# Four feed-forwards in two phases: all up tiles, then all down tiles with 512-column products over eight banks

## The chip, the core and the metric

The kernel runs on one core of a Trainium2 chip. A core has a matrix engine (TensorE), VectorE, ScalarE, GpSimd, and SyncE, which here issues the loads. The time is the device time of one execution in microseconds. A smaller time is better.

## What is computed

Two transformer blocks on 256 tokens of width 1024, in f32. The first has two gated feed-forwards (inner width 2816), a mixer of several attentions and a cross attention to a memory; the second has an RWKV-7 layer and a windowed attention, each with a squared-ReLU feed-forward (inner width 4096). Cut to what matters here:

```python
def swiglu(h, w_gate, w_up, w_down):
    return (jax.nn.silu(h @ w_gate) * (h @ w_up)) @ w_down

def squared_relu_mlp(h, w1, w2):
    return jnp.square(jax.nn.relu(h @ w1)) @ w2

def first_block(...):
    x = x + 0.5 * swiglu(rmsnorm(x, ffn1_norm), ffn1_w_gate, ffn1_w_up, ffn1_w_down)
    x = x + hybrid_mixer(rmsnorm(x, mix_norm), ...)
    x = x + memory_cross_attention(rmsnorm(x, mem_q_norm), rmsnorm(mem, mem_kv_norm), ...)
    x = x + 0.5 * swiglu(rmsnorm(x, ffn2_norm), ffn2_w_gate, ffn2_w_up, ffn2_w_down)
    return rmsnorm(x, final_norm)

def second_block(...):
    for i in range(2):
        out = rwkv7_time_mix(...) if i == 0 else swa_layer(rms_norm(x, ln_mix[1]), k_sh, v_sh, ...)
        x = x + out
        x = x + squared_relu_mlp(rms_norm(x, ln_mlp[i]), mlp_w1[i], mlp_w2[i])
        if i == 0:
            k_sh, v_sh = shared_kv(x, kv_norm, w_kv, k_gain)
    return x

```

## The kernel before

All activations stand transposed on chip: 128 channels on the partitions, 8 chunks of channels (`KC`), 256 tokens (`SEQ`) along the free axis. All weights come as one stream of 1 MB tiles of 128 x 2048 f32, in the order of use, through a ring of four (`feed`, L266, on SyncE's queue). A matmul reads `fp32r`, which keeps only a part of the bits, so every operand is split in two: ScalarE copies half a tile to `tile_hi` (L305, `heads_after`), VectorE subtracts to `tile_lo` (L315, `rests_after`). Four halves have room (`SPLIT`); a half is split again when TensorE has used the half four before. `may_split` decides from the tile number that a call is given how far a splitter may go at that place, so the calls `heads_before`, `rests_after` and the like are what sets the order of both engines.

`product` (L353 to L357) makes one product of a 128 x 128 weight block with 256 tokens in three matmuls of 256 columns: high by high, high weights by low activations, low weights by high activations. Each matmul loads its own weights. A tile holds 16 products.

`ffn_stage` runs four times: `ffn1` and `ffn2` (gated, 22 up tiles and 11 down tiles), `mlp1` and `mlp2` (squared ReLU, 16 and 16). A step `j` makes 256 inner values: one up tile (`col_to_T`; gated: two) into a PSUM bank. In the gated stages VectorE multiplies by the token scale (L768, L771), ScalarE applies SiLU (L726), VectorE multiplies both (L774). In the others ScalarE applies ReLU (L731) and VectorE scales (L780) and squares (L781). Then ScalarE writes the high part (L736), VectorE the low part (L789). They go to one of three slots (`depth`), of which the first begins at another offset (`AT_FIRST_SLOT` 128, the others `AT_MOVING` 160, modulo 256 bytes). The down tile of step `j` comes `LAG` = 2 steps later (`row_to_T`) and adds into banks 4 to 7, two chunks of 256 columns in each:

```python
            for j in range(steps):
                ...
                if j >= LAG:
                    down(j - LAG)
            mark_tail(e)
            for j in range(steps - LAG, steps):
                down(j)
```

The last down tile finishes the output chunks pair by pair. `tail_vector` adds each pair to the residual in one operation (L514, or L516 with the factor 0.5), ScalarE writes the high part for the next stage (L548) and the squares (L554), VectorE the low part (L524). `first_to_T` of the next stage waits for two chunks at a time (`x_arrives`), then `scale_sums` and `scale_spread` bring the token scale in.

## Time and profile before

| what | value |
|---|---|
| median of 3 runs | 1413.38 us (1409.81 to 1413.94) |
| the profiled execution, span | 1422.4 us |
| TensorE busy (matmul) | 1372.8 us, 97% |
| VectorE busy | 913.7 us, 64% |
| ScalarE busy | 706.0 us, 50% |
| HBM read | 219.55 MB, 155 GB/s over the span |
| matmuls | 12692 |

The profiled execution has no other time of its own than the span, from the first to the last instruction; it is 9.0 us above the median of the runs. Matmuls overlap in the records (one lasts 280 ns and the next starts 113 to 118 ns later), so a busy TensorE says little, and starts are what to compare.

### The profile page before, as it was taken

The page shows a single profiled execution, that of the slowest core. Times are in us where ns is not written, and L with a number is a line of the kernel's source. Part 1 is how long each engine was busy: PE and PEld are TensorE (multiplying, and loading weights), DVE is VectorE, ACT ScalarE, POOL GpSimd, SP SyncE. Part 2 cuts the span into 40 slices and gives each one's busy share as a digit, 9 for nine tenths or more (in the row PEclk, how much of TensorE's full clock was granted, in tenths as well). Part 3 has the DMA queues.
Part 4 walks back from the last instruction along what each step waited for, and adds up shares of the span by engine and source line. Part 5 has one row for each costly group of instructions (what it writes and reads, how often), then busy time and mean ns, then how long its engine had stood idle before and what let it go on. Part 6 is the DMA issues. An engine that isn't in the chain of part 4 may idle for free. (4 is left out here: it accounts for less than half of the span.)

```text
span 1422.4 us, 28871 instructions
## 1 busy us (share of the span) xinstructions
PE 1372.8 (97%) x12692; PEld 1314.1 (92%) x12692; DVE 913.7 (64%) x1419; ACT 706.0 (50%) x1098; POOL 8.2 (1%) x14
## 2 busy tenths in 40 slices
PE   7999999999899999999999899999999996999999
PEld 7999999888799999999998677889999995999999
DVE  4665566557785546666588763667666668666664
ACT  5444455356564446444458333446444466554442
POOL 0000000000000000000000010000000000000000
PEclk9999999999999999999999998999999999999999
DMA  7555555461344344655524021114555541255552
GB/s 272 208 179 191 194 180 179 182 264 60 119 178 178 129 151 156 214 182 197 199 85 176 31 91 60 61 60 167 190 197 207 190 149 60 94 204 178 178 184 84
DMA packets 33109, 222.48 MB, mean 156 GB/s; under 512 B 3879, under 2 KB 5295, under 8 KB 6616
## 3 DMA queue, kind: packets, MB, share of 16 engines
q1 hardware_dynamic: 31928, 219.57, 42.7%
q8 instruction: 100, 1.64, 0.4%
q10 hardware_dynamic: 1056, 1.07, 0.2%
q14 instruction: 25, 0.20, 0.0%
HBM read 219.55 MB, written 1.07 MB: 155 GB/s over the span
## 5 line engine op out<-in xcount | busy, mean ns | idle before, releaser
L315 DVE TENSOR_TENSOR tile_lo<-ring,tile_hi 128x1024 fp32r<-128x1024 f32 x388 | 466.0, 1222 | 276.8 <-ACT tile_hi L305 276.2
L305 ACT ACTIVATE tile_hi<-ring 128x1024 fp32r<-128x1024 f32 x388 | 399.5, 1053 | 250.8 <-PE ps L357 245.8
L355 PE MATMUL ps<-hT_hi,tile_hi 128*128 128x256 f32 x1664 | 467.5, 281 | 5.0 <-DVE tile_lo L315 1.8
L356 PE MATMUL ps<-hT_lo,tile_hi 128*128 128x256 f32 x1664 | 463.4, 278 | 0.0
L357 PE MATMUL ps<-hT_hi,tile_lo 128*128 128x256 f32 x1664 | 463.4, 278 | 0.0
L355 PEld LDWEIGHTS ps<-hT_hi,tile_hi 128*128 128x128 f32 x1664 | 315.0, 189 | 10.6 <-issue 4.6
L356 PEld LDWEIGHTS ps<-hT_lo,tile_hi 128*128 128x128 f32 x1664 | 312.9, 188 | 0.0
L357 PEld LDWEIGHTS ps<-hT_hi,tile_lo 128*128 128x128 f32 x1664 | 312.7, 188 | 0.0
L355 PE MATMUL ps<-hidden_hi,tile_hi 128*128 128x256 f32 x864 | 241.2, 279 | 0.0
L357 PE MATMUL ps<-hidden_hi,tile_lo 128*128 128x256 f32 x864 | 241.2, 279 | 0.0
L356 PE MATMUL ps<-hidden_lo,tile_hi 128*128 128x256 f32 x864 | 241.2, 279 | 0.0
L355 PEld LDWEIGHTS ps<-hidden_hi,tile_hi 128*128 128x128 f32 x864 | 163.5, 189 | 0.0
L356 PEld LDWEIGHTS ps<-hidden_lo,tile_hi 128*128 128x128 f32 x864 | 162.4, 188 | 0.0
L357 PEld LDWEIGHTS ps<-hidden_hi,tile_lo 128*128 128x128 f32 x864 | 162.3, 188 | 0.0
L736 ACT ACTIVATE hidden_hi<-hidden_whole 128x512 fp32r<-128x512 f32 x54 | 34.2, 633 | 114.1 <-DVE hidden_whole L774 65.8
L789 DVE TENSOR_TENSOR hidden_lo<-hidden_whole,hidden_hi 128x512 fp32r<-128x512 f32 x54 | 37.4, 692 | 39.3 <-ACT hidden_hi L736 26.2
L780 DVE TENSOR_TENSOR hidden_whole<-gate,token_scale 128x512 f32<-128x512 f32 x32 | 22.1, 692 | 32.4 <-ACT gate L731 32.4
L731 ACT ACTIVATE gate<-ps 128x512 f32<-128x512 f32 x32 | 19.0, 595 | 42.8 <-PE ps L357 42.8
L1064 ACT ACTIVATE scores<-scores,lane_stats 128x128 f32<-128x128 f32 (+3 forms) x80 | 35.4, 445 | 8.8 <-DVE lane_stats L1090 8.8
L355 PE MATMUL ps<-y_turned,tile_hi 128*128 128x256 f32 x128 | 35.8, 280 | 2.9 <-DVE tile_lo L315 2.9
L726 ACT ACTIVATE gate<-gate 128x512 f32<-128x512 f32 x22 | 13.9, 632 | 46.1 <-DVE gate L768 46.1
L356 PE MATMUL ps<-y_turned,tile_hi 128*128 128x256 f32 x128 | 35.4, 277 | 0.0
(467 smaller groups left out, 1997.5 us busy)
## 6 DMA issues: line engine op xcount, KB each, us to landing
ring<-stream SPq DMA_DIRECT2D x204, 1024.0 KB, 4.8
x_sb<-x SPq DMA_DIRECT2D x4, 256.0 KB, 4.0
bias<-f_dram ACTq DMA_DIRECT2D x1, 1024.0 KB, 8.1
fox_bias<-forget_dram SPq DMA_DIRECT2D x1, 1024.0 KB, 6.2
squares<-mem SPq DMA_DIRECT2D x1, 1024.0 KB, 4.7
out<-x_sb SPq DMA_DIRECT2D x4, 256.0 KB, 2.2
const_sb<-const SPq DMA_DIRECT2D x1, 581.0 KB, 9.8
small_sb<-small SPq DMA_DIRECT2D x1, 493.5 KB, 9.5
```

What stands on the lines that cost most here:

```text
L305: act.activation(e.w_hi[:, n % SPLIT, :], e.ring[:, tile % RING, span(n % 2, HALF)], ACT.Copy).then_inc(e.tile_hi.handle, 1)
L315: dve.tensor_tensor(e.w_lo[:, n % SPLIT, :], e.ring[:, CUT[n // 2] % RING, span(n % 2, HALF)], e.w_hi[:, n % SPLIT, :].bitcast(F32), ALU.s ...
L355: pe.matmul(out, left[0], right[0], start=start, stop=False)
L356: pe.matmul(out, left[0], right[1], start=False, stop=False)
L357: return pe.matmul(out, left[1], right[0], start=False, stop=stop)
L726: act.activation(tmp[:, j % 2, :], tmp[:, j % 2, :], ACT.Silu).then_inc(*act_done.one())
L731: act.activation(tmp[:, j % 2, :], e.ps[:, up_bank(j, 0), :], ACT.Relu).then_inc(*act_done.one())
L736: act.activation(slot(0, j), whole[:, j % 2, :], ACT.Copy).then_inc(*hi_ready.one())
L780: link.done(dve.tensor_tensor(halves_of(both), halves_of(tmp[:, j % 2, :]), scale_pairs(e), ALU.mult))
L789: dve.tensor_tensor(slot(1, j), both, slot(0, j).bitcast(F32), ALU.subtract).then_inc(*hidden_ready.one())
L1064: x = act.activation(summed(step)[:, lane], summed(step)[:, lane], ACT.Exp, bias=st[:, 0, lane:lane + 1], accum_out=st[:, 1, lane:lane + 1])
```

## The change

- Each feed-forward now runs all its up tiles and then all its down tiles, in the program and in the weight stream (`lay_out_stream`).
- The inner values of all steps stay on chip, in one tensor `hidden` at `AT_MOVING`, the high and low part of a step 2048 bytes apart.
- A down product is `wide_product`: one matmul of 512 columns (high weights by both parts of the activations) and one of 256 (low weights by the high part). Each of the 8 output chunks has a PSUM bank of its own, whose halves are summed at the end.
- The residual add therefore takes two operations per pair of chunks, the second waiting for the first.
- Up tiles rotate over four banks; the first down tile takes the banks in the order in which they were last used. `mlp2` starts its rotation at bank 4 (`first=2`). The key, value and query products after `mlp1` move to other banks.
- Pairs of high and low parts are now one tensor each with views (`Pair`), so `tile_hi` and `tile_lo` are `tile_pair`, `hT_hi` and `hT_lo` are `hT_pair`.

```diff
+    return pe.matmul(out, left.lo, right.hi, start=False, stop=stop)
+
+
+def wide_product(pe, bank, left, right, start, stop):
+
+
+
+    def low(stop):
+        return pe.matmul(bank[:, 0:SEQ], left.lo, right.hi, start=False, stop=stop)
+
+    if stop:
+        low(False)
+    mm = pe.matmul(halves_of(bank), left.hi, right.both, start=start, stop=stop)
+    return mm if stop else low(False)
 
 
...
-def add_to_residual(e, dve, b, scale, last_tile, bank=4):
+def add_to_residual(e, dve, b, scale, last_tile, bank=4, wide=False):
 
     if b < 3:
         dve.wait_ge(*e.sig("acc_ready").since(b + 1))
     else:
         multiplied(e, dve, last_tile)
+    if wide:
+        xs = e.x[:, two(b), :]
+        for half in range(2):
+            x = dve.scalar_tensor_tensor(out=xs, in0=e.ps[:, pair_of(b), span(half, SEQ)], scalar=scale, in1=xs,
+                                         op0=ALU.mult, op1=ALU.add)
+            if half == 0:
+                Chain(dve, e.sig("dve_step")).done(x)
+        x.then_inc(*e.sig("residual_added").one())
+        return
     xs = e.x[:, two(b), :].rearrange("p m n -> p (m n)")
     if scale == 1.0:
...
+def pair_of(n, first=0):
+
+    at = 2 * ((n + first) % 4)
+    return slice(at, at + 2)
+
+
+def bank_of(m, first=0):
+    return pair_of(m // 2, first).start + m % 2
+
...
+            first_to_T(e, pe, g0, hT, up_bank(0))
+            col_to_T(e, pe, g0 + 1, hT, up_bank(1), between=lambda: scale_sums(e, pe, scale_bank))
+            scale_spread(e, pe, scale_bank)
+            for n in range(2, count):
+                if n >= 4:
+                    pe.wait_ge(*emptied.at(n - 3))
+                col_to_T(e, pe, g0 + n, hT, up_bank(n))
+
+            def down(w, k, j, m, start=False, stop=False):
+                return wide_product(pe, e.ps[:, bank_of(m), :], cut(w, ALL, span(m, P)), chunk(j, k), start, stop)
+
+            halves = [arrived(e, pe, down0, k) for k in range(2)]
+            pe.wait_ge(*hidden_ready.at(1))
+            up_last = [max([-1] + [n for n in range(count) if up_bank(n) == bank_of(m)]) for m in range(KC)]
+            for m in sorted(range(KC), key=lambda m: up_last[m]):
+                pe.wait_ge(*(emptied.at(up_last[m] + 1) if up_last[m] >= 0 else e.sig("scale_ready").at(1)))
+                for k in range(2):
+                    mm = down(halves[k], k, 0, m, start=k == 0)
+            mm.then_inc(*e.tile_done.one(2))
+            for j in range(1, steps - 1):
                 pe.wait_ge(*hidden_ready.at(j + 1))
-                row_to_T(e, pe, down_tile(j), hid[j % depth], 0, j == 0, j == steps - 1)
-
-            for j in range(steps):
-                if gated and j >= 2:
-
-                    pe.wait_ge(*hidden_ready.at(j - 1))
-                if not gated and j >= 4:
-
-                    pe.wait_ge(*act_done.at(j - 3))
-                for which in range(per - 1):
-                    nth = (per - 1) * j + which
-                    if nth == 0:
-                        first_to_T(e, pe, up_tile(j, which), hT, up_bank(j, which))
-                    elif nth == 1:
-                        col_to_T(e, pe, up_tile(j, which), hT, up_bank(j, which), between=lambda: scale_sums(e, pe, 7))
-                        scale_spread(e, pe, 7)
-                    else:
-                        col_to_T(e, pe, up_tile(j, which), hT, up_bank(j, which))
-                if j >= LAG:
-                    down(j - LAG)
+                for k in range(2):
+                    w = arrived(e, pe, down0 + j, k)
+                    for m in range(KC):
+                        mm = down(w, k, j, m)
+                    mm.then_inc(*e.tile_done.one())
             mark_tail(e)
-            for j in range(steps - LAG, steps):
-                down(j)
+            pe.wait_ge(*hidden_ready.at(steps))
+            halves = [arrived(e, pe, end, k) for k in range(2)]
+            for m in range(KC):
+                for k in range(2):
+                    mm = down(halves[k], k, steps - 1, m, stop=k == 1)
+                if m % 2 == 1 and m < KC - 1:
+                    mm.then_inc(*e.sig("acc_ready").one())
+            mm.then_inc(*e.tile_done.one(2))
 
         @block.scalar
         def _(act):
             heads_after(e, act, 2 * (g0 + 1))
             scale_root(e, act)
-            scale_copy(e, act, 7)
+            scale_copy(e, act, scale_bank)
+
...
+                    tile_after(e, act, g0 + j)
                     if j >= 2:
...
+                heads_after(e, act, 2 * (g0 + ups * (j + 1)))
                 act.wait_ge(*whole_ready.at(j + 1))
...
-                both = whole[:, j % 2, :]
+                rests_before(e, dve, g0 + ups * j + 1)
...
+                    dve.tensor_tensor(gate[:, j % 2], halves_of(e.ps[:, up_bank(2 * j), :]), scale_pairs(e),
+                                      ALU.mult).then_inc(*consumed.one())
+                    rests_after(e, dve, 2 * (g0 + 2 * j) + 2)
+                    tile_after(e, dve, g0 + 2 * j + 1)
+                    dve.tensor_tensor(whole[:, j % 2], halves_of(e.ps[:, up_bank(2 * j + 1), :]), scale_pairs(e),
+                                      ALU.mult).then_inc(*consumed.one())
+                    dve.wait_ge(*consumed.at(2 * j + 2))
                     dve.wait_ge(*act_done.at(j + 1))
-                    x = dve.tensor_tensor(both, both, tmp[:, j % 2, :], ALU.mult)
+                    dve.tensor_tensor(whole[:, j % 2], whole[:, j % 2], gate[:, j % 2], ALU.mult).then_inc(*whole_ready.one())
...
+                    link.done(dve.tensor_tensor(whole[:, j % 2], gate[:, j % 2], scale_pairs(e), ALU.mult))
+                    dve.tensor_tensor(whole[:, j % 2], whole[:, j % 2], whole[:, j % 2], ALU.mult).then_inc(*whole_ready.one())
+                rests_after(e, dve, 2 * (g0 + ups * (j + 1)))
                 dve.wait_ge(*hi_ready.at(j + 1))
...
     link = Chain(e.nc.vector, e.sig("dve_step"))
     KEYS = -1
-    banks = {KEYS: 0, 0: 1, 1: 2, 2: 7, 3: 5}
...
 
     heads_of = lambda n: 2 if n == KEYS else 4
@@ -3241,8 +3283,8 @@
             act.activation(s.q[:, PAIRS, :], e.ps[:, 0, 0:SEQ], ACT.Copy)
             act.activation(s.key_squares[:, :], e.ps[:, 0, 0:SEQ], ACT.Square).then_inc(*squared.one())
             return
-        act.activation(flat(s.q[:, two(n), :]), e.ps[:, 1 + n, :], ACT.Copy)
-        act.activation(flat(e.sq[:, two(n), :]), e.ps[:, 1 + n, :], ACT.Square).then_inc(*squared.one())
+        act.activation(flat(s.q[:, two(n), :]), e.ps[:, query_bank[n], :], ACT.Copy)
+        act.activation(flat(e.sq[:, two(n), :]), e.ps[:, query_bank[n], :], ACT.Square).then_inc(*squared.one())
 
     def sums_at(n):
         return e.ps[:, 7 if n == KEYS else 6, span(order[n], TT * 4)].rearrange("p (t h) -> p t h", t=TT)[:, :, 0:heads_of(n)]
...
-        tiles.extend(downs[-LAG:])
+        tiles.extend(downs)
 
     def cols(w, columns=None):
         tiles.extend(col_tiles(w, np.arange(w.shape[1]) if columns is None else columns))
```

TensorE, ffn1, the place where the first down tile begins. Before (step 0's down tile, behind the sixth up tile):

```order
L355 MATMUL ps<-hT_hi,tile_hi 128x256
L356 MATMUL ps<-hT_lo,tile_hi 128x256
L357 MATMUL ps<-hT_hi,tile_lo 128x256
L355 MATMUL ps<-hidden_hi,tile_hi 128x256
L356 MATMUL ps<-hidden_lo,tile_hi 128x256
L357 MATMUL ps<-hidden_hi,tile_lo 128x256
L355 MATMUL ps<-hidden_hi,tile_hi 128x256
L356 MATMUL ps<-hidden_lo,tile_hi 128x256
L357 MATMUL ps<-hidden_hi,tile_lo 128x256
```

After (behind the 22nd up tile; L386 is the wide matmul, L382 the low one, L372 to L374 are `product`):

```order
L372 MATMUL ps<-hT_pair,tile_pair 128x256
L373 MATMUL ps<-hT_pair,tile_pair 128x256
L374 MATMUL ps<-hT_pair,tile_pair 128x256
L386 MATMUL ps<-hidden,tile_pair 128x512
L382 MATMUL ps<-hidden,tile_pair 128x256
L386 MATMUL ps<-hidden,tile_pair 128x512
L382 MATMUL ps<-hidden,tile_pair 128x256
```

Three matmuls of 256 columns for each product have become one of 512 and one of 256.

VectorE, the middle of mlp2: the hidden operations (L780, L781, L789; after: L832, L833, L836) and the splits of weight tiles (L315; after: L331). Before:

```order
L315 TENSOR_TENSOR tile_lo<-ring,tile_hi 128x1024 x4
L780 TENSOR_TENSOR hidden_whole<-gate,token_scale 128x512
L781 TENSOR_TENSOR hidden_whole<-hidden_whole 128x512
L789 TENSOR_TENSOR hidden_lo<-hidden_whole,hidden_hi 128x512
L315 TENSOR_TENSOR tile_lo<-ring,tile_hi 128x1024 x4
L780 TENSOR_TENSOR hidden_whole<-gate,token_scale 128x512
L781 TENSOR_TENSOR hidden_whole<-hidden_whole 128x512
L789 TENSOR_TENSOR hidden_lo<-hidden_whole,hidden_hi 128x512
```

After:

```order
L331 TENSOR_TENSOR tile_pair<-ring,tile_pair 128x1024
L832 TENSOR_TENSOR hidden_whole<-gate,token_scale 128x512
L833 TENSOR_TENSOR hidden_whole<-hidden_whole 128x512
L331 TENSOR_TENSOR tile_pair<-ring,tile_pair 128x1024
L836 TENSOR_TENSOR hidden<-hidden_whole,hidden 128x512
L331 TENSOR_TENSOR tile_pair<-ring,tile_pair 128x1024
L832 TENSOR_TENSOR hidden_whole<-gate,token_scale 128x512
L833 TENSOR_TENSOR hidden_whole<-hidden_whole 128x512
L331 TENSOR_TENSOR tile_pair<-ring,tile_pair 128x1024
L836 TENSOR_TENSOR hidden<-hidden_whole,hidden 128x512
L331 TENSOR_TENSOR tile_pair<-ring,tile_pair 128x1024
```

A step had four splits, for its up and its down tile; it now has two, one of them ahead of the low part, and the splits of all down tiles come behind the last step.

VectorE, the end of ffn1: residual adds (L516; after: L547) and low parts of the next input (L524; after: L565). Before:

```order
L315 TENSOR_TENSOR tile_lo<-ring,tile_hi 128x1024 x5
L516 SCALAR_TENSOR_TENSOR x_sb<-ps,x_sb 128x512 x3
L524 SCALAR_TENSOR_TENSOR hT_lo<-x_sb,small_sb,hT_hi 128x256 x2
L516 SCALAR_TENSOR_TENSOR x_sb<-ps,x_sb 128x512
L524 SCALAR_TENSOR_TENSOR hT_lo<-x_sb,small_sb,hT_hi 128x256 x6
L315 TENSOR_TENSOR tile_lo<-ring,tile_hi 128x1024 x2
```

After:

```order
L331 TENSOR_TENSOR tile_pair<-ring,tile_pair 128x1024 x20
L547 SCALAR_TENSOR_TENSOR x_sb<-ps,x_sb 128x512 x6
L565 SCALAR_TENSOR_TENSOR hT_pair<-x_sb,small_sb,hT_pair 128x256 x2
L547 SCALAR_TENSOR_TENSOR x_sb<-ps,x_sb 128x512 x2
L565 SCALAR_TENSOR_TENSOR hT_pair<-x_sb,small_sb,hT_pair 128x256 x6
L331 TENSOR_TENSOR tile_pair<-ring,tile_pair 128x1024 x2
```

The splits of all eleven down tiles stand in a row ahead of the adds, and each add has become two.

## Rows read from the trace of the kernel before

**Rows 1.** The page, part 1: busy us, share of the span, instructions.

```profile
PE 1372.8 (97%) x12692; PEld 1314.1 (92%) x12692; DVE 913.7 (64%) x1419; ACT 706.0 (50%) x1098; POOL 8.2 (1%) x14
```

**Rows 2.** Waits of TensorE: us in total, times, longest us.

```profile
PE ps L355 <- DVE tile_lo L315: 7.0, 8, 1.5
```

**Rows 3.** Timeline, TensorE, stage mlp1: start us, us.

```profile
1069.92 0.28 PE L355 MATMUL ps<-hidden_hi,tile_hi 128*128 128x256 f32 x1
...
1074.00 0.28 PE L355 MATMUL ps<-hidden_hi,tile_hi 128*128 128x256 f32 x1
...
1080.12 0.28 PE L355 MATMUL ps<-hidden_hi,tile_hi 128*128 128x256 f32 x1
...
1084.34 0.28 PE L355 MATMUL ps<-hidden_hi,tile_hi 128*128 128x256 f32 x1
```

**Rows 4.** Timeline, TensorE, stage ffn1.

```profile
118.02 0.28 PE L355 MATMUL ps<-hidden_hi,tile_hi 128*128 128x256 f32 x1
...
122.26 0.28 PE L355 MATMUL ps<-hidden_hi,tile_hi 128*128 128x256 f32 x1
```

**Rows 5.** Windows of ffn1, ffn2, mlp1, mlp2: us, busy (x) by engine, PEclk, DMA.

```profile
100.00:140.00 40.00, 40.00 (x342) 40.00 (x341) 24.66 (x26) 17.11 (x19) 0.00 (x0) 1.00 0.52 185
640.00:680.00 40.00, 40.00 (x354) 40.00 (x353) 24.07 (x24) 16.84 (x19) 0.00 (x0) 1.00 0.58 210
1040.00:1080.00 40.00, 40.00 (x353) 40.00 (x352) 25.59 (x26) 19.10 (x22) 0.00 (x0) 1.00 0.55 197
1320.00:1360.00 40.00, 40.00 (x341) 40.00 (x340) 23.33 (x25) 18.20 (x22) 0.00 (x0) 1.00 0.53 194
```

**Rows 6.** Timeline, TensorE, stage mlp2.

```profile
1263.29 0.28 PE L357 MATMUL ps<-hT_hi,tile_lo 128*128 128x256 f32 x1
1263.46 0.38 PE L355 MATMUL ps<-hT_hi,tile_hi 128*128 128x256 f32 x1
```

**Rows 7.** Timeline, TensorE, the key/value tile after mlp1.

```profile
1143.07 0.33 PE L355 MATMUL ps<-kvT_hi,tile_hi 128*128 128x256 f32 x1
...
1144.09 0.33 PE L355 MATMUL ps<-kvT_hi,tile_hi 128*128 128x256 f32 x1
```

**Rows 8.** Timeline, TensorE, memory projection.

```profile
427.79 0.41 PE L357 MATMUL ps<-memT_hi,tile_lo 128*128 128x256 f32 x1
...
428.86 0.41 PE L356 MATMUL ps<-memT_lo,tile_hi 128*128 128x256 f32 x1
```

**Rows 9.** Window around it.

```profile
427.00:431.00 4.00, 4.00 (x23) 4.00 (x23) 1.67 (x4) 0.71 (x2) 0.00 (x0) 0.58 0.72 262
```

**Rows 10.** Groups by line and form, TensorE: xcount, busy us, mean ns.

```profile
L1817 PE MATMUL ps<-mem_kv,fox_bias 128*128 128x256 f32 x32 | 7.1, 381 | 0.8 <-ACT fox_bias L1855 0.8
...
L1281 PE MATMUL ps<-bias,flip_sb 128*128 128x512 f32 x8 | 3.6, 592 | 0.0
```

**Rows 11.** The page, part 5, VectorE.

```profile
L315 DVE TENSOR_TENSOR tile_lo<-ring,tile_hi 128x1024 fp32r<-128x1024 f32 x388 | 466.0, 1222 | 276.8 <-ACT tile_hi L305 276.2
...
L780 DVE TENSOR_TENSOR hidden_whole<-gate,token_scale 128x512 f32<-128x512 f32 x32 | 22.1, 692 | 32.4 <-ACT gate L731 32.4
```

**Rows 12.** Timeline, VectorE, two hidden operations of ffn1.

```profile
101.22 0.69 DVE L771 TENSOR_TENSOR hidden_whole<-ps,token_scale 128x512 f32<-128x512 f32 x1 [0.45 <-PE ps L357]
101.95 0.69 DVE L774 TENSOR_TENSOR hidden_whole<-hidden_whole,gate 128x512 f32<-128x512 f32 x1
```

**Rows 13.** Timeline, ScalarE's last split and VectorE's adds, end of ffn1.

```profile
197.44 1.06 ACT L305 ACTIVATE tile_hi<-ring 128x1024 fp32r<-128x1024 f32 x1 [1.73 <-PE ps L357]
...
199.68 1.28 DVE L516 SCALAR_TENSOR_TENSOR x_sb<-ps,x_sb 128x512 f32<-128x512 f32 x2
...
202.29 0.87 DVE L524 SCALAR_TENSOR_TENSOR hT_lo<-x_sb,small_sb,hT_hi 128x256 fp32r<-128x256 f32 x2
```

**Rows 14.** Timeline, TensorE, first matmul after ffn1.

```profile
203.31 0.36 PE L355 MATMUL ps<-hT_hi,tile_hi 128*128 128x256 f32 x1 [0.25 <-DVE hT_lo L524]
```

**Rows 15.** Timeline, VectorE, last add of ffn2.

```profile
717.45 0.69 DVE L516 SCALAR_TENSOR_TENSOR x_sb<-ps,x_sb 128x512 f32<-128x512 f32 x1 [0.67 <-PE ps L357]
```

More of the change, by code:

```diff
@@ L368, in cut @@
 def cut(pair, *index):
-    return tuple(part[index] for part in pair)
+    both = None if pair.both is None else pair.both[(index[0], slice(None), *index[1:])]
+    return Pair(pair.hi[index], pair.lo[index], both)
 ALL = slice(None)
@@ L656, in ffn_stage @@
     steps = width // 256
-    per = 3 if gated else 2
+    ups = 2 if gated else 1
     g0 = FIRST[section]
-    depth = 3
-    act_done, whole_ready, hi_ready, hidden_ready, scaled, chain = (
-        e.sig(x) for x in ("gate_ready", "hidden_whole_ready", "hidden_hi_ready", "hidden_ready", "gate_scaled", "dve_step"))
-    hT = e.hT
-    def up_tile(j, which):
-        return g0 + (per - 1) * j + max(j - LAG, 0) + which
-    def down_tile(j):
-        return g0 + (per - 1) * min(j + LAG + 1, steps) + j
@@ L670, in up_bank @@
-    def up_bank(j, which):
-        return 2 * (j % 2) + which if gated else (0, 2, 1, 3)[j % 4]
-    end = down_tile(steps - 1)
+    count = ups * steps
+    down0, end = g0 + count, g0 + count + steps - 1
+    consumed, act_done, whole_ready, hi_ready, hidden_ready, chain = (
+        e.sig(x) for x in ("gate_scaled", "gate_ready", "hidden_whole_ready", "hidden_hi_ready", "hidden_ready", "dve_step"))
+    emptied = consumed if gated else act_done
+    hT = e.hT
+    scale_bank = bank_of(4, first)
@@ L675, in ffn_stage, with chunk @@
     all_squared = e.sig("squared").since(4)
+    up_bank = lambda n: bank_of(n % 4, first)
     with Open(nc) as block, ExitStack() as stack:
-        hid = [e.pair(stack, f"hidden{n}", [P, 2, SEQ], AT_MOVING if n else AT_FIRST_SLOT) for n in range(depth)]
-        whole = e.sb(stack, f"hidden_whole{nc.next_id()}", [P, 2, 2 * SEQ])
-        tmp = e.sb(stack, f"gate{nc.next_id()}", [P, 2, 2 * SEQ])
-        def slot(part, j):
-            return hid[j % depth][part][:, :, :].rearrange("p m n -> p (m n)")
+        hidden = e.sb(stack, f"hidden{nc.next_id()}", [P, steps, 2, 2, SEQ], F32R, AT_MOVING)
+        whole = e.sb(stack, f"hidden_whole{nc.next_id()}", [P, 2, 2, SEQ])
+        gate = e.sb(stack, f"gate{nc.next_id()}", [P, 2, 2, SEQ])
+        def chunk(j, c):
+            return Pair(hidden[:, j, 0, c, :], hidden[:, j, 1, c, :], hidden[:, j, :, c, :])
```

119 lines of the change are left out of this document (50 added, 69 removed).

## The prediction

> **What bounds the kernel now.** I read the page first. TensorE is busy 97% of the span, VectorE 64%, ScalarE 50% [rows 1]. Busy time says little of pipelined matmuls, so I asked the waits next: inside the four feed-forwards TensorE waits for almost nothing (8 waits for a split tile, 7.0 us in the whole program [rows 2]). The bound there is the rhythm of the matmuls themselves, and the timeline gives it. I take starts of equal matmuls, 12 products (36 matmuls) apart.
>
> That shows **two rhythms at one clock**. In the first squared-ReLU stage 12 products take 4.08 us: 340.0 ns a product, 113.3 ns a matmul [rows 3]. In the first gated stage the same instructions take 4.24 us: 353.3 ns, 117.8 ns a matmul [rows 4]. Windows of 40 us, one per stage, tell which stage runs how: about 342 matmuls is the slow rhythm, 354 the fast one, all at clock 1.00, that is 2.4 GHz [rows 5]. So ffn1 and mlp2 were slow, ffn2 and mlp1 fast. The rhythm changes only where TensorE stops for a moment: in mlp2 it went from fast to slow at 1263.46 after a hiccup of some 60 ns [rows 6]. I call it a draw, made anew at each stop. Products from hidden slot 0, which lies at another offset, take 351.7 ns in a fast stage (4.22 us for 12) [rows 3]; in a slow one they hardly stand out.
>
> **Why 113 and not 107?** 256 columns at 2.4 GHz are 106.7 ns. In the key/value tile, three matmuls of 256 columns alternate with six of 128: nine take 1.03 us, 114 ns each, though their columns would need 71 ns on average [rows 7]. Their one common cost is a weight load each. And where a stream is long enough to cover a load, the surcharge goes: at 427 us, at half clock, matmuls of 256 columns stand 214 ns apart (1.07 us for 5), which is 256 columns at 1.2 GHz and nothing more [rows 8, 9]. So a load of 128 columns takes about 111 to 114 ns, and a 256-column stream at full clock just fails to cover it.
>
> **The change part by part.** *Wide down products.* Each of 864 down products (11, 11, 16, 16 tiles of 16) drops one weight load and one instruction; columns stay 768. The 512-column matmul should cost its stream, 214 ns by [rows 8], since it covers the next load. The low one keeps 113.3. Together 328 ns. The bounds: 320 (768 columns at 2.4 GHz) below, and above 353.3, if 512 columns cost two slow matmuls. Far off stands the one 512-column row of this kernel, plain f32: it lasts 592 ns, one of 256 columns 381 [rows 10]. 211 ns for 256 columns more would make 422 of 512, but that is twice the fp32r rhythm already at 256, so I read from it only that time goes with columns. I take 328, by the row that is nearest in mechanism. By stage, from this profile: ffn1 176 products x 25.3 = 4.5 us; ffn2 112 x 12.0 + 64 of slot 0 x 23.7 = 2.9; mlp1 160 x 12.0 + 96 x 23.7 = 4.2; mlp2 256 x 25.3 = 6.5. **Sum -18.1 us.** In the fast stages slot 0's penalty (64 x 11.7 = 0.7 and 96 x 11.7 = 1.1 us) is part of it, as every hidden part now lies at the good offset.
> The Trainium skill ("TensorE: Matmul & The Clock Gate", on the measured gap) states N/2.4 + 2.5 ns back to back: 216 and 109, a product of 325 and a sum of -20.7. It would have today's product at 328, and the rows say 340 to 353, so the measurement decides.
>
> *Up tiles in a row.* Same matmuls, same tiles, same bytes (a 1 MB tile per 5.4 to 5.7 us). VectorE has the tighter budget in the squared-ReLU stages: before, three hidden operations per 11 us, now per 5.4. Two splits (1.22 us) and three operations (0.69) are 4.5 us, and the ReLU must be awaited some 0.85 us after the tile's end: 5.3 of 5.4 us [rows 11]. The split awaited is needed a whole tile later, so I cost it at nothing; the cover is 5.4 us of slack, and if it went, each of 32 tiles would show a stop. The gated stages use 7.3 of 11 us. TensorE's waits on emptied banks are for a tile three back: nothing. The first down tile takes the banks last used for up products last, 4 us after the final up matmul: nothing. The stop of the gated stages in their fourth tile stays: the split that ends it still stands behind the first step's hidden operations.
>
> *Down tiles in a row.* Both splitters have only 2.4 us of work per 5.3: nothing.
>
> *The tail.* Here the change costs. The residual add is now two dependent 128x512 operations per pair of chunks: 0.73 us to a dependent one [rows 12], 0.59 to an independent (two end after 1.28) [rows 13], so 1.32 us against 0.69. TensorE delivers a pair every 4 x 0.328 = 1.31 us. In ffn1 VectorE comes out of its last split 2.24 us after ScalarE began its half (197.44 to 199.68) [rows 13], and ScalarE begins when the slot is freed, one tile (now 5.25 us) before TensorE's end T: free at T-3.0. Three adds to T+0.95, the two rests (0.87 for both, the next may enter after 0.8) [rows 13] to T+1.75, and TensorE starts the next stage 0.15 later, as it does now: T+1.9. Today it starts 0.25 us after its last matmul [rows 14]: +1.65. Then add four (to T+3.05) and the second rests (T+3.85) come before chunk 2, which is wanted 1.4 us after the start, at T+3.3: +0.65. **ffn1 +2.3.** mlp1 has the same start, but its next tile takes 2.06 us for two chunks [rows 7], which hides the second wait: **+1.65**. In ffn2 all downstream hangs on add four: it would end at T+2.3, today at about T+0.75, since it begins at TensorE's last matmul and takes 0.69 [rows 15]: **+1.5**. In mlp2 no split stands ahead, the adds keep pace, and the end moves by one operation: **+0.65**. Sum +6.1 us; bounds 0, if the next stage hides it all, and 8, if the norms behind it wait too.
>
> Everything else (banks in the projections after mlp1, the layout of the pairs, the order of tiles in HBM) moves no instruction: nothing.
>
> **Sum: -18.1 + 6.1 = -12.0** against this execution: 1422.4 to 1410.4. The median of the runs shown is 1413.38, 9.0 us below this span. About 2000 matmuls at the fast instead of the slow rhythm (4.5 ns each) would make that. If so, the timed runs have fewer slow stages; with all four fast the products give back 14.2 (twice 2.9 and twice 4.2) and the net is -8.1. I take a value between, nearer the second, -9.4: **1404.0 us**.
>
> **The rivals.** (1) *Forecast*, up phases about as today: 1400 to 1408; chance 0.47. (2) *The draws fall well*: 3648 up matmuls stand in four uninterrupted runs; two more of these fast, 1056 and 768 matmuls x 4.5 ns, are -8: 1396. Speaks for it: fewer handovers, fewer stops. Chance 0.18. (3) *The draws fall badly*: the same +8, or the up phase of mlp2 keeps being stopped by VectorE's narrow budget: 1412, no change to be told. 0.22. (4) *The change doesn't do what it says*: the chip may run 512 columns as two matmuls with a load each. The place is the down product, the price two slow matmuls for the wide one, 353.3 ns, against an average of 348.9 today (328 + 18.1 us / 864): +3.8 us, and the tail's 6.1 stays: 1423. It decides from a product of 342 ns on (348.9 less 6.1 us / 864). Against it speaks that loads are written per instruction; no fp32r row has 512 columns. 0.11. (5) *The clock*: it was 0.58 on average from 427 to 431 us [rows 9], behind a run of one-column matmuls. If the down phases ran so, a product would take 768 columns / 1.2 = 640 ns: 864 x 0.291 = +252 us, and 1672 with the tail. Today's products already go round four banks at clock 1.00 [rows 5]. 0.02. The Trainium skill ("TensorE: Matmul & The Clock Gate", "A second HAM failure mode: psum-queue depth-cycling") speaks against this change: it saw 512-column matmuls that went round the banks lose the full clock again and again.
>
> **How the numbers follow.** A measurement here tells 0.3%, 4.2 us: faster is below 1409.1, slower above 1417.6. Faster: nearly all of (1), (2) and a little of (3), 0.66. Same: 0.23. Slower: (4), 0.11. The range takes (1), (2) and most of (3): 1394 to 1414, with about 0.2 outside.
>
> **What would show it.** A wide matmul 213 to 217 ns long from start to start and a low one at 113 (or 118) confirm the term; 227 or more breaks it. Tail: TensorE's stop after ffn1 at 1.5 to 2 us and a second one of 0.7 after two chunks. Windows of 40 us in the up phases: 342 or 354 matmuls, which is the draw. Stops between up tiles of mlp1 or mlp2 on a split tile would show that VectorE's budget is too narrow, which I cost at nothing. I am wrong if the wide matmul saves no load, or if the clock leaves 1.00 in a down phase.

## The result, and the profile after

The changed kernel takes **1424.22 us** (median of 4 runs, 1422.42 to 1427.71), the kernel before on the same chip 1413.66 (4 runs, 1409.81 to 1416.64): ratio 1.0075, interval 1.0048 to 1.0101. It is slower by 0.75%; 1404.0 was forecast, with a range of 1394 to 1414. The time is nearly that of the fourth rival, 1423. The profiled execution has a span of 1422.9 us. All executions but three of the kernel before (1432.60, 1434.36 and 1432.11 us, over 1.5% above its fastest on their chip) count as undisturbed, and its ranges below and all ratios go by those.

The page, part 1, and its costliest matmuls of the down products (L386 is the wide matmul, L382 the low one), against [rows 1]:

```profile
PE 1368.5 (96%) x11828; PEld 1270.1 (89%) x11828; DVE 918.6 (65%) x1435; ACT 712.5 (50%) x1098; POOL 8.2 (1%) x14
...
L386 PE MATMUL ps<-hidden,tile_pair 128*128 128x512 f32 x864 | 303.3, 397 | 0.0
L382 PE MATMUL ps<-hidden,tile_pair 128*128 128x256 f32 x864 | 237.5, 281 | 0.0
```

The 864 instructions and loads are gone, as the change says. The time is not. The timeline of TensorE in the down phase of ffn1 (start us, us) tells why:

```profile
159.84 0.40 PE L386 MATMUL ps<-hidden,tile_pair 128*128 128x512 f32 x1
160.07 0.28 PE L382 MATMUL ps<-hidden,tile_pair 128*128 128x256 f32 x1
160.19 0.40 PE L386 MATMUL ps<-hidden,tile_pair 128*128 128x512 f32 x1
...
161.96 0.40 PE L386 MATMUL ps<-hidden,tile_pair 128*128 128x512 f32 x1
```

From 159.84 to 161.96 are six products in 2.12 us: **353.3 ns each**, over the whole phase 235.0 for the wide matmul and 118.3 for the low one. That is the slow rhythm of [rows 4] to the tenth of a nanosecond. All four down phases have it. Windows of 40 us, up and down phases of each stage in turn, against [rows 5] (busy and count by engine, then TensorE's clock):

```profile
60.00:100.00 40.00, 40.00 (x355) 40.00 (x354) 27.51 (x30) 19.96 (x23) 0.00 (x0) 1.00 0.59 208
150.00:190.00 40.00, 40.00 (x228) 34.73 (x228) 17.15 (x14) 14.85 (x14) 0.00 (x0) 1.00 0.55 184
600.00:640.00 40.00, 40.00 (x356) 40.00 (x355) 26.89 (x29) 19.13 (x22) 0.00 (x0) 1.00 0.56 187
660.00:700.00 40.00, 40.00 (x228) 34.73 (x227) 17.15 (x14) 15.27 (x15) 0.00 (x0) 1.00 0.57 187
1000.00:1040.00 40.00, 40.00 (x355) 40.00 (x355) 31.38 (x37) 23.58 (x30) 0.00 (x0) 1.00 0.57 199
1080.00:1120.00 40.00, 40.00 (x228) 34.72 (x228) 17.58 (x15) 14.85 (x14) 0.00 (x0) 1.00 0.55 185
1280.00:1320.00 40.00, 40.00 (x356) 40.00 (x355) 31.83 (x38) 24.08 (x30) 0.00 (x0) 1.00 0.59 204
1340.00:1380.00 40.00, 40.00 (x228) 34.77 (x227) 17.15 (x14) 15.18 (x15) 0.00 (x0) 1.00 0.58 200
```

Two matmuls make a product now, so 228 in 40 us are 114 products of 351 to 353 ns; a product of 340 would have shown 235. The up phases run at 355 matmuls, all fast. The weight loads are busy 34.7 us of 40 and no longer all the time: the load has slack, and the product gains nothing by it. The clock is 1.00 throughout.

The tail came as forecast. TensorE and VectorE at the end of ffn1, against [rows 13] and [rows 14]:

```profile
198.03 0.39 PE L386 MATMUL ps<-hidden,tile_pair 128*128 128x512 f32 x1
200.12 0.36 PE L372 MATMUL ps<-hT_pair,tile_pair 128*128 128x256 f32 x1 [1.70 <-DVE hT_pair L565]
...
201.49 0.28 PE L374 MATMUL ps<-hT_pair,tile_pair 128*128 128x256 f32 x1
202.15 0.39 PE L372 MATMUL ps<-hT_pair,tile_pair 128*128 128x256 f32 x1 [0.37 <-DVE hT_pair L565]
```

```profile
195.13 4.06 DVE L547 SCALAR_TENSOR_TENSOR x_sb<-ps,x_sb 128x512 f32<-128x512 f32 x6
199.10 0.87 DVE L565 SCALAR_TENSOR_TENSOR hT_pair<-x_sb,small_sb,hT_pair 128x256 fp32r<-128x256 f32 x2
199.89 1.41 DVE L547 SCALAR_TENSOR_TENSOR x_sb<-ps,x_sb 128x512 f32<-128x512 f32 x2
```

Six of the eight adds stand in a row before the first rest operation, so TensorE starts the next stage 2.09 us after its last matmul, where it needed 0.53 before. It stops again after two chunks for the same reason (0.66 us between two starts): the last two adds come between the rests.

One thing was not foreseen. TensorE's waits for a split tile, against [rows 2]:

```profile
PE ps L372 <- DVE tile_pair L331: 5.5, 6, 1.5
```

Two of the eight are gone, 1.5 us: the stops in the fourth tile of the two gated stages.

### The profile page after: what moved, and what is told of

Same layout as the page of the kernel before. It is cut to its first block and busy times, and to the rows that moved or that the text cites. A ratio compares the mean times of both kernels' runs of the same rounds, so it can differ in the third digit from the quotient of the medians.

```text
span 1422.9 us, 27161 instructions
## 1 busy us (share of the span) xinstructions
PE 1368.5 (96%) x11828; PEld 1270.1 (89%) x11828; DVE 918.6 (65%) x1435; ACT 712.5 (50%) x1098; POOL 8.2 (1%) x14
## 5 line engine op out<-in xcount | busy, mean ns | idle before, releaser
L331 DVE TENSOR_TENSOR tile_pair<-ring,tile_pair 128x1024 fp32r<-128x1024 f32 x388 | 470.1, 1222 | 319.4 <-ACT tile_pair L321 316.9
L321 ACT ACTIVATE tile_pair<-ring 128x1024 fp32r<-128x1024 f32 x388 | 405.2, 1057 | 324.0 <-PE ps L382 168.1
L372 PE MATMUL ps<-hT_pair,tile_pair 128*128 128x256 f32 x1664 | 464.4, 279 | 5.4 <-DVE hT_pair L565 2.9
L373 PE MATMUL ps<-hT_pair,tile_pair 128*128 128x256 f32 x1664 | 460.4, 277 | 0.0
L374 PE MATMUL ps<-hT_pair,tile_pair 128*128 128x256 f32 x1664 | 460.4, 277 | 0.0
L372 PEld LDWEIGHTS ps<-hT_pair,tile_pair 128*128 128x128 f32 x1664 | 312.7, 188 | 10.9 <-issue 6.2
L374 PEld LDWEIGHTS ps<-hT_pair,tile_pair 128*128 128x128 f32 x1664 | 312.8, 188 | 0.0
L373 PEld LDWEIGHTS ps<-hT_pair,tile_pair 128*128 128x128 f32 x1664 | 312.6, 188 | 0.0
L386 PE MATMUL ps<-hidden,tile_pair 128*128 128x512 f32 x864 | 303.3, 397 | 0.0
L382 PE MATMUL ps<-hidden,tile_pair 128*128 128x256 f32 x864 | 237.5, 281 | 0.0
L386 PEld LDWEIGHTS ps<-hidden,tile_pair 128*128 128x128 f32 x864 | 160.4, 188 | 37.1
L382 PEld LDWEIGHTS ps<-hidden,tile_pair 128*128 128x128 f32 x864 | 162.2, 188 | 2.6
L791 ACT ACTIVATE hidden<-hidden_whole 128x512 fp32r<-128x512 f32 x54 | 34.2, 634 | 37.8 <-DVE hidden_whole L833 24.2
L832 DVE TENSOR_TENSOR hidden_whole<-gate,token_scale 128x512 f32<-128x512 f32 x32 | 22.1, 691 | 27.4 <-ACT gate L788 27.4
L372 PE MATMUL ps<-y_turned,tile_pair 128*128 128x256 f32 x128 | 35.8, 280 | 2.9 <-DVE tile_pair L331 2.9
L836 DVE TENSOR_TENSOR hidden<-hidden_whole,hidden 128x512 fp32r<-128x512 f32 x54 | 37.0, 685 | 1.4 <-ACT hidden L791 1.4
L374 PE MATMUL ps<-y_turned,tile_pair 128*128 128x256 f32 x128 | 35.4, 277 | 0.0
L373 PE MATMUL ps<-y_turned,tile_pair 128*128 128x256 f32 x128 | 35.4, 277 | 0.0
```

The source lines that it names most:

```text
L321: act.activation(e.w.hi[:, n % SPLIT, :], e.ring[:, tile % RING, span(n % 2, HALF)], ACT.Copy).then_inc(e.tile_hi.handle, 1)
L331: dve.tensor_tensor(e.w.lo[:, n % SPLIT, :], e.ring[:, CUT[n // 2] % RING, span(n % 2, HALF)], e.w.hi[:, n % SPLIT, :].bitcast(F32), ALU.s ...
L372: pe.matmul(out, left.hi, right.hi, start=start, stop=False)
L373: pe.matmul(out, left.hi, right.lo, start=False, stop=False)
L374: return pe.matmul(out, left.lo, right.hi, start=False, stop=stop)
L382: return pe.matmul(bank[:, 0:SEQ], left.lo, right.hi, start=False, stop=stop)
```

## The experiments

Three questions: is it the wide matmul, or the phases, that holds the down products at 353.3 ns; what in a matmul takes the time, load or stream; and does the rest of the loss belong to the doubled additions? Ratios are to the kernel before, run on the same chip in the same session.

**1. The kernel before, a second trace.**

> The kernel before, unchanged, for a second trace. Theory A (the rhythm is drawn anew at each stop of TensorE): about 1413 us, and in this execution other stages than ffn1 and mlp2 show the slow rhythm; its span is nearer to 1412 than to 1422. Theory B (the rhythm belongs to the place in the program): again ffn1 and mlp2 at 342 matmuls per 40 us, the others at 354, span about 1422.

Measured: 1418.41 us (1412.84 to 1424.56, 12 runs), ratio 0.999 (0.996 to 1.002): on this chip the kernel before takes some 5 us more than on the first. The span is 1414.2. The two fences show windows in ffn1, ffn2 and mlp2, first of this execution, then of the one profiled before:

```profile
80.00:180.00 100.00, 100.00 (x882) 100.00 (x881) 61.57 (x62) 44.55 (x49) 0.00 (x0) 1.00 0.54 191
600.00:680.00 80.00, 80.00 (x681) 80.00 (x681) 46.70 (x47) 34.92 (x39) 0.00 (x0) 1.00 0.53 189
...
1270.00:1370.00 100.00, 100.00 (x879) 100.00 (x879) 63.21 (x64) 47.29 (x54) 0.00 (x0) 1.00 0.54 196
```

```profile
80.00:180.00 100.00, 100.00 (x850) 100.00 (x850) 59.49 (x59) 43.08 (x47) 0.00 (x0) 1.00 0.52 185
600.00:680.00 80.00, 80.00 (x705) 80.00 (x704) 49.66 (x50) 34.99 (x39) 0.00 (x0) 1.00 0.56 197
...
1270.00:1370.00 100.00, 100.00 (x850) 100.00 (x850) 60.88 (x63) 45.92 (x53) 0.00 (x0) 1.00 0.53 190
```

ffn1 and mlp2 turned fast, ffn2 slow. Theory B is out: the rhythm is drawn in each execution, stage by stage. The place still sets the odds. In the nine traces of kernels with phases (the kernel after and the variants below), the up phases of ffn1 and ffn2 are fast every time, that of mlp1 in three, that of mlp2 in seven.

The draw explains a part of the spread of the runs. The kernel before took 1410.86 to 1429.30 us on this chip and 1409.57 to 1429.74 on the next; its 6240 feed-forward matmuls (3648 up, 2592 down) at 4.5 ns between the rhythms are 28 us. There is a second part outside the feed-forwards. The kernel after was traced three times. In the first and the third trace (experiment 10) all up phases are fast, and the four stages, from the start of their first matmul to that of their last, add up to 723.9 and 723.8 us. The spans are 1422.9 and 1427.7 all the same, and TensorE stood at half clock for 38.9 and 55.0 us (mean granted clock 0.986 and 0.981), all of it outside the feed-forward stages. So a difference of 5 us between two single executions proves nothing about the feed-forwards; their own stretches do.

**2. The wide matmul split in two.**

```diff
-    mm = pe.matmul(halves_of(bank), left.hi, right.both, start=start, stop=stop)
+    pe.matmul(bank[:, 0:SEQ], left.hi, right.hi, start=start, stop=False)
+    mm = pe.matmul(bank[:, SEQ:512], left.hi, right.lo, start=False, stop=stop)
```

> The kernel after, with each 512-column matmul written as two of 256 columns into the two halves of the same bank: one weight load and one instruction more per down product, all else equal. Theory A (time goes with the columns streamed, loads are hidden): the product stays within 340 to 353 ns, 1413 to 1424 us. Theory B (a load binds at 256 columns and the wide matmul saves one but pays for its two separate runs): the split product is 340 to 353 as well, but the wide one would then owe its 353.3 to its two runs. Theory C (the wide matmul did save something): the product rises above 353.3, by up to 113 ns, 1424 to 1520 us.

Measured: 1418.96 us (1409.84 to 1425.35, 12 runs), ratio 0.9987 (0.9958 to 1.0016). In its ffn1 (timeline, TensorE) three products take 1.02 us, 340 ns each:

```profile
160.13 0.28 PE L386 MATMUL ps<-hidden,tile_pair 128*128 128x256 f32 x1
160.24 0.28 PE L387 MATMUL ps<-hidden,tile_pair 128*128 128x256 f32 x1
160.36 0.28 PE L382 MATMUL ps<-hidden,tile_pair 128*128 128x256 f32 x1
...
161.15 0.28 PE L386 MATMUL ps<-hidden,tile_pair 128*128 128x256 f32 x1
```

With the load put back the product is **faster** than without it in both gated down phases, 340, and as slow, 353.3, in the other two. A load that a 256-column stream covers costs nothing here. In each stage the down phase has the rhythm of the up phase ahead of it. That holds for all twelve down phases of narrow products in the traces of experiments 2, 3 and 11. The kernel after and that of experiment 12, which has the same products, have 353.3 in all sixteen traced down phases, though fourteen of their up phases are fast: the wide matmul takes no part in the draw. Theory C is out.

**3. The phases alone.** All three matmuls of a product go to one half of the bank, and one addition is left.

```diff
-    if stop:
-        low(False)
-    mm = pe.matmul(halves_of(bank), left.hi, right.both, start=start, stop=stop)
-    return mm if stop else low(False)
+    return product(pe, bank[:, 0:SEQ], left, right, start, stop)
...
-        for half in range(2):
+        x = dve.scalar_tensor_tensor(out=xs, in0=e.ps[:, pair_of(b), 0:SEQ], scalar=scale, in1=xs,
```

> The kernel after with down products of three 256-column matmuls that all add in one half of the bank, and one residual addition per pair of chunks instead of two: the order of up and down phases alone. If the wide matmul is what costs: product 340.0 ns where the rhythm is fast, 864 x 13.3 = 11.5 us less than after, the doubled addition's 6.1 us back too: 1424.2 - 17.6 = 1406.6. If the down phase is slow for another reason (its order, the two rows of banks, the hidden layout): 353.3 stays, and only the 6.1 us come back: 1418.

Measured: 1413.78 us (1404.70 to 1420.11, 12 runs), ratio **0.996** (0.9931 to 0.9989). The forecast of 1406.6, counted from another chip's times, is missed by 7 us; against the kernel before it meant 7 us less, and 5.6 were measured. Its profiled execution, span 1406.0, has fast down phases in three stages and a slow one in mlp1, behind a slow up phase. Down windows of ffn1 and mlp1:

```profile
150.00:190.00 40.00, 40.00 (x355) 40.00 (x354) 17.52 (x16) 15.94 (x15) 0.00 (x0) 1.00 0.54 189
1080.00:1120.00 40.00, 40.00 (x342) 40.00 (x341) 17.16 (x14) 15.28 (x15) 0.00 (x0) 1.00 0.53 189
```

So neither the order in phases nor the eight banks make a down phase slow; the wide matmul does.

**4. Matmuls by themselves.** A kernel of 18 to 36 matmuls in a row, each pattern four times behind a handshake.

> Leaves the whole computation out (it copies x to the output) and times matmuls of fp32r alone, 18 to 36 in a row per pattern, each four times, with a handshake with VectorE ahead of each. Theory A (columns): 512 columns take twice what 256 take (226 to 236 ns), 128 columns about half, one weight repeated changes nothing. Theory B (a load of about 111 ns binds): 64, 128 and 192 columns all take 111 to 114 ns, 512 columns 213 to 216 if in one run. The run of two separate pieces against one contiguous run of 512: equal if the layout is no part of it. Offsets: narrow at 128 takes 117 ns, at 160 113 ns, by the rows of slot 0 of the kernel before.

Measured in one execution. Timeline rows of TensorE: a row's time is that of the whole run of matmuls. In turn: wide and low alternating, the wide one in two pieces; the same in one contiguous run; 18 of 512 columns in two pieces; 64 columns at full clock (first row of that pattern) and at half; 18 of 512 columns with one weight; 18 of 512 at byte 224.

```profile
54.81 4.49 PE L105 MATMUL ps<-moving,weights 128*128 128x512 f32 x24 [0.51 <-DVE z L99]
...
74.41 4.49 PE L105 MATMUL ps<-moving,weights 128*128 128x512 f32 x24 [0.51 <-DVE z L99]
...
93.89 4.46 PE L105 MATMUL ps<-moving,weights 128*128 128x512 f32 x18 [0.51 <-DVE z L99]
98.64 1.64 PE L105 MATMUL ps<-moving,weights 128*128 128x64 f32 x13 [0.29 <-DVE z L99]
...
119.26 7.89 PE L105 MATMUL ps<-moving,weights 128*128 128x64 f32 x36 [0.51 <-DVE z L99]
...
354.51 4.46 PE L105 MATMUL ps<-moving,weights 128*128 128x512 f32 x18 [0.51 <-DVE z L99]
...
418.25 4.37 PE L105 MATMUL ps<-moving,weights 128*128 128x512 f32 x18 [0.29 <-DVE z L99]
```

From start to start, in the steady part: **64 columns 111.7 ns** at full clock, 192 columns 111.7, 256 columns 113.3 or 117.8, 320 146.7, 384 173 to 177, 448 202.3, **512 columns 233.3**, with one weight 233.3, in two pieces 233.3, at byte 224 226.6. Wide and low together: 353.3, joined or not. (128 columns were caught only at half clock: 213.3 ns.) So both theories held half: there is a floor of 111.7 ns, and it binds at 64 and 192 columns. From 256 on the stream binds, and it is slower than its columns: 213.3 ns would be 512 columns at 2.4 GHz. Layout and repeated weights are no part of it. I call the floor the load's, because every matmul here has a load of its own, also where the weight repeats, and the load's record lasts 192 ns in fp32r against 98 in bf16 (experiment 8), where there is no such floor. No run leaves a load out, so that reading is argued and not shown.

**5, 6, 7. The kernel after again, with the hidden values at another offset, and in another order.**

```diff
-        hidden = e.sb(stack, f"hidden{nc.next_id()}", [P, steps, 2, 2, SEQ], F32R, AT_MOVING)
+        hidden = e.sb(stack, f"hidden{nc.next_id()}", [P, steps, 2, 2, SEQ], F32R, 224)
```

```diff
-    if stop:
+    if stop or low_first:
         low(False)
...
-                        mm = down(w, k, j, m)
+                        mm = down(w, k, j, m, low_first=m % 2 == 1)
```

> The kernel after, unchanged, on one chip with the two variants below. Theory D (the stream of 512 columns itself is slower than columns / 2.4 GHz: 233.3 ns alone in the fourth run, with one weight or many, in one run or two): all four down phases again at 353.3 ns a product, whatever the rhythm of the up phases, 1420 to 1430 us.

> The kernel after with the hidden values at byte 224 of 256 instead of 160. In the fourth run 512 columns took 226.6 ns there and 233 at the other offsets, but three 256-column matmuls took 360 there and 340 at 160. Theory D with the offset of each stream apart: 226.6 + 113.3 to 120 = 340 to 347 ns a product, 5 to 11 us less than the kernel after. If the offset matters only for matmuls of one length in a row: 353.3, no change. If the low matmul suffers more: 360, 6 us more.

> The kernel after with every second product of a down tile written low first: wide, low, low, wide, wide, low, low, wide. In the last down tile of the kernel after, where this order stands already, two products take 0.69 us instead of 0.707. Theory E (the change from one length to the other costs some ns): 347 ns a product, 864 x 6 = 5 us less. Theory D: 353.3 or, where the fast rhythm sets in, 340 to 347.

Measured, 10 runs each: 1426.52 us (1421.54 to 1428.95), ratio 1.004 (1.0012 to 1.0068); 1426.54 (1416.15 to 1434.73), 1.0022 (0.9981 to 1.0064); 1423.35 (1416.83 to 1435.16), 1.0025 (0.9985 to 1.0064). The traces tell more than these spreads. Down windows of mlp1 and mlp2 with the other offset, then of mlp1 in the other order:

```profile
1080.00:1120.00 40.00, 40.00 (x228) 34.68 (x227) 17.57 (x15) 14.84 (x14) 0.00 (x0) 1.00 0.55 185
1340.00:1380.00 40.00, 40.00 (x233) 35.24 (x232) 19.00 (x16) 15.26 (x16) 0.00 (x0) 1.00 0.54 185
```

```profile
1080.00:1120.00 40.00, 40.00 (x233) 35.11 (x232) 17.93 (x15) 14.83 (x14) 0.00 (x0) 1.00 0.54 185
```

The kernel after shows 353.3 in its four down phases again (D holds). At byte 224 three of four phases have some 347 ns, in the other order all four. So the order saves 6 ns a product, as E forecast; that the number of changes is what counts is not shown (see experiment 8). No variant with a wide matmul reached the 340 of three narrow ones. The gain in time, at most 5 us, does not stand out from the draws.

**8. bf16, and half clock.**

> Leaves the whole computation out (it copies x to the output). The wide product at eight offsets of its moving data, with its lo part at other offsets than its hi part, in both orders; bf16 matmuls of 64 to 512 columns; and matmuls of 512, 256 and 384 columns straight behind 100 of 64 columns, which in the fourth run brought the clock down. Theory D as a limit in reading the moving data: bf16 of 512 columns takes 213 to 216 ns where fp32r takes 226 to 235, and at half clock fp32r of 512 columns takes 427, its columns and no more. Theory F (a fixed cost per column in the array or in PSUM): bf16 takes 226 to 235 too, and 453 at half clock.

Measured in one execution. Rows in turn: bf16 of 256, 512, 128 and 64 columns. The second fence is the tile view of the moving data in a stretch at clock 0.50 (count, ns, first and last start, form).

```profile
332.65 4.10 PE L101 MATMUL ps<-moving_bf,weights_bf 128*128 128x256 bf16 x36 [0.52 <-DVE z L95]
...
341.46 4.06 PE L101 MATMUL ps<-moving_bf,weights_bf 128*128 128x512 bf16 x18 [0.36 <-DVE z L95]
...
362.73 2.18 PE L101 MATMUL ps<-moving_bf,weights_bf 128*128 128x128 bf16 x36 [0.52 <-DVE z L95]
...
370.17 1.22 PE L101 MATMUL ps<-moving_bf,weights_bf 128*128 128x64 bf16 x36 [0.52 <-DVE z L95]
```

```profile
L101 PE MATMUL ps<-moving,weights x5: 628/628/628, 391.1 to 392.8; 128*128 128x512 f32 x5
```

bf16 runs at 109.2 ns for 256 columns and 216 for 512, start to start, and at 29 for 64, each with its own load: no load floor near 111 ns, and 2.5 ns above the columns. fp32r of 512 columns at half clock stands 426.7 ns apart (five starts from 391.1 to 392.8), of 256 columns 213.3: the columns and nothing more. So the surcharge of 13 to 22 ns on 512 columns belongs to four-byte data at full clock, and theory F is out. That fits a limit in reading the operands; which part of the chip sets it was not tried. The Trainium skill ("TensorE: Matmul & The Clock Gate", "Wait — 56ns, not 53.3ns?") gives N/2.4 + 2.5 ns; bf16 agrees within half a nanosecond, fp32r does not.

The wide product at eight offsets, the hi and lo parts apart, and both orders: 346 to 355 ns. Byte 160, the place in the kernel after, is among the worst: 353.2 to 353.4 in all four repetitions, and 346.8 there with the other order. At bytes 0 and 128 all four have 346.6 to 346.8 in the old order. At byte 224 it is 352 to 354, where the kernel of experiment 6 had 347 in three phases; why they differ is open. So either a better place or the other order gives 347, and nothing gives 340.

**9. Which offset, and is it a draw?**

> Leaves the whole computation out (it copies x to the output). The narrow product, three 256-column matmuls, with its moving data at every fourth byte from 128 to 192 of 256 and its lo part elsewhere than its hi part, six times each behind VectorE operations of different lengths. The rhythm as a matter of the offset alone: each offset has one figure, the same in all six repetitions. The rhythm as a draw at the start of a run: 340.0 and 353.3 both occur at byte 160, as in the fourth run (three and one of four). If some offset gives 340 in all six, a kernel could have the fast rhythm always: up to 4.4 ns for each of its 6240 feed-forward matmuls, 28 us; the timed runs of the kernel before, 1409.6 to 1434.4 on one chip, spread about as much.

Measured in one execution: at byte 160, the place in both kernels, two of the six repetitions in the timeline:

```profile
278.50 4.37 PE L85 MATMUL ps<-moving,weights 128*128 128x256 f32 x36 [0.32 <-DVE z L79]
283.34 4.51 PE L85 MATMUL ps<-moving,weights 128*128 128x256 f32 x36 [0.47 <-DVE z L79]
```

Five took 340.0 ns a product, one 353.3. Of the 16 other offsets byte 156 had 346.7 in three of six and 360 in the others, and the rest lie at 350 to 370; the lo part elsewhere gives 353 to 360. So byte 160 (with weights at 224) is the best place tried and the only one with 340, and there the start of a run of matmuls decides between 340.0 and 353.3. No offset gives 340 always. What in the start decides it is open.

**10, 11, 12. On one chip: after, the phases alone, and after with one addition.** The last has the additions of experiment 3 with the products of the kernel after.

> The kernel after once more, on one chip with the two kernels below and with more runs. All down phases at 353.3 ns a product; the up phases at 340 or 353.3 by draw (3648 up matmuls x 4.4 ns = 16 us between the best and the worst): 1421 to 1432 us.

> The third run's kernel (order of phases, narrow products, one addition), now beside the kernel after. It should be 6.1 us less by the tails, and 0 to 11.5 us less by the down products (11.5 where all of its down phases draw the fast rhythm, 0 where all draw the slow one): with half of them fast 12 us less than the kernel after, 1412 to 1416 us, and below the kernel before.

> The kernel after with the second residual addition left out, so that the products of the hidden values' lo part, which lie in the other half of each bank, never reach the output: that part of the computation is left out. The doubled addition alone: 6.1 us less than the kernel after (ffn1 2.3, ffn2 1.5, mlp1 1.65, mlp2 0.65), 1416 to 1425 us. If TensorE's stop behind ffn1 has another cause than the additions, it stays at about 2 us.

| kernel | median us (range, runs) | ratio, interval |
|---|---|---|
| after | 1428.39 (1420.08 to 1431.51, 6) | 1.0086, 1.0054 to 1.0118 |
| phases alone | 1409.14 (1400.52 to 1417.34, 12) | 0.9954, 0.9925 to 0.9982 |
| after, one addition | 1419.02 (1413.06 to 1426.91, 12) | 1.0028, 1.0005 to 1.0050 |

TensorE at the end of ffn1 with one addition (timeline):

```profile
197.68 0.39 PE L386 MATMUL ps<-hidden,tile_pair 128*128 128x512 f32 x1
198.35 0.35 PE L372 MATMUL ps<-hT_pair,tile_pair 128*128 128x256 f32 x1 [0.28 <-DVE hT_pair L562]
```

0.67 us from start to start where the kernel after has 2.09, and the second stop (0.66 from 201.49) is gone. Between the two traces the additions cost 1.42 + 0.54 in ffn1, 1.42 in mlp1 (2.09 against 0.67), 0.7 in mlp2 (last start to the end, 4.2 against 3.5) and about 1.2 in ffn2 (6.02 against 4.82 us from the last wide matmul to the norm's spread): 5.3 us. The medians differ by 9.4, with draws and the clock outside the feed-forwards between them: the six runs of the kernel after go from 1431.51 us at a mean granted clock of 0.981 down to 1420.08 at 0.993.

The phases alone take 19.3 us less than the kernel after, where 12 were forecast, and lie below the range of 1412 to 1416. The two traces are 26.0 us apart (1427.7 and 1401.7). Of these 10.7 lie in the four stages (723.8 against 713.2, all rhythms fast in the second), 5.3 in the tails, and 10 elsewhere, where the first stood 55.0 us at half clock and the second 27.8. So 16 us of it belong to the change. The kernel of the phases alone is the best of all here, below the kernel before on two chips.

## Why the prediction was wrong

**The step that failed** is "*The 512-column matmul should cost its stream, 214 ns by [rows 8], since it covers the next load*". It costs 235.0, the product 353.3 instead of 328, and the term is not -18.1 us. Against this profile's own average of 348.9 it is +3.8 us; against four fast stages, whose average with slot 0 is 344.3 (340 + 320 x 11.7 / 864), +7.8; against four slow ones nothing. Two readings led there, and each was true of something else:

- The floor is real (111.7 ns at 64 and 192 columns). In the key/value tile [rows 7] it would account for the six matmuls of 128 columns, a size not measured alone at full clock. The 256-column stream happens to take 113.3, 1.6 ns more, by its own limit. Two causes lay within 2% of each other, and I gave the time to the one I could take away.
- The 214 ns at half clock [rows 8, 9] did not show that a covered load sheds the surcharge. At half clock a load takes 213 ns as well (64 columns: 7.89 us for 36 matmuls), and the surcharge goes with the clock, at 512 columns too.

**Rhythms and draws**: right, and shown by the second trace of before. The step from span to the median of the runs (9.0 us, put down to the draws alone) is right only in part. The two traces of before are 8.1 us apart (1422.4 and 1414.2); 5.1 of that lie in the four stages and 3.0 outside them. And "I take 328" gave the wide product no rhythm, while it has always 353.3 or, in another order or place, 347.

**The tail**: +6.1 forecast, 5.3 measured between the traces of experiments 10 and 12: ffn1 2.0 for 2.3, mlp1 1.4 for 1.65, ffn2 1.2 for 1.5, mlp2 0.7 for 0.65. The mechanism and each place were right.

**Phases at nothing**: right for the budgets, since no up tile of mlp1 or mlp2 waits for a split. Wrong in one sentence, that the stop of the gated stages in their fourth tile stays: both are gone, 1.6 us (0.93 less a matmul's 0.12, twice). What the phases give back besides is slot 0, 320 x 11.7 ns = 3.7 us when all stages are fast. Together 5.3 us; measured were 0.40% and 0.46%, 5.7 and 6.5 us, in experiments 3 and 11. The prediction had slot 0 inside the term of the wide products, but the new place of the hidden values earns it without them.

**The rivals**: (4) had the right price and place, but for a mechanism that did not occur as told: the loads are saved (1728 in the down products where there were 2592). It is two slow matmuls' worth of streaming. That its 1423 came so near the 1424.22 is in part luck, since the same kernel took 1428.39 on another chip. Its chance of 0.11 was too small. The far row [rows 10], of which I kept only that time goes with columns, said as much about the fp32r stream as it could. (5) the clock stayed at 1.00 in every down window. The loss of clock of which the Trainium skill ("TensorE: Matmul & The Clock Gate", "A second HAM failure mode: psum-queue depth-cycling") tells is not there.

**The sum after the fact**, against the profiled execution: 1422.4 + 3.8 (products) + 5.3 (tails) - 1.6 (stops) - 8.2 (the 1824 up matmuls of ffn1 and mlp2, slow before and fast now, 4.5 ns each) = 1421.7; the span is 1422.9. The parts outside the feed-forwards differ by more than that between two executions of one kernel, so the agreement within 1.2 us is partly luck. The sum also tells why this span hardly moved while the median rose by 10.6: the trace of before had two slow up phases that the trace of after had not. With all rhythms fast the four stages take 719.2 us in the kernel before (each stage from the trace where it was fast), 713.2 with the phases alone and 723.9 in the kernel after: 6.1 us less by the phases and 10.7 more by the wide products. With the tails that is 10.0 more than before.

## What to carry to other kernels

Where two costs overlap, a time that equals one of them proves nothing about it; find a row, or measure a few dozen matmuls alone, at a size where the two part (64 and 512 columns here), before a change is built that removes one. In fp32r a 512-column matmul was no cheaper than two of 256 columns here (235.0 ns against 226.6 to 235.6), and accumulating its parts in two halves of a bank is paid for on VectorE at the tail, where every operation stands on the path. When a change has two parts, judge them apart: the phases alone gain 0.4 to 0.5%, and the wide products spend more than that. And compare the stretches that a change touches, one rhythm with the same rhythm, before the times of whole executions.

## What the runs showed of the hardware

- fp32r matmuls at full clock, start to start, each with a weight load: 64 and 192 columns 111.7 ns, 256 113.3 or 117.8, 512 226.6 to 235.0. At half clock 213.3 for 64, 128 and 256 columns and 426.7 for 512 (experiments 4 and 8). bf16: 29, 56, 109.2 and 216 ns for 64, 128, 256 and 512.
- The time of an fp32r stream depends on where the moving data start within 256 bytes, and on the weights' offset beside it: with moving data at 160 a product took 340 with weights at 224, 353.3 with 96, 356 with 32, 360 with 160; with both at 224 also 360. Equal distances gave equal times in these pairs (experiment 4).
- At the best offset two rhythms exist for three narrow matmuls, 340.0 and 353.3, and a run keeps the one it starts with: in twelve of twelve stages with narrow down products it went from the up phase through the down phase.
- In experiment 4 the clock went from 1.00 to 0.50 during fp32r matmuls of 64 columns in a row, stayed there through those of 128, and rose again at 192.
